# Latent attention: two heads' weighted sums side by side, probabilities scaled on GpSimd

## The reference, cut to what matters

```python
def block(i):
    start = i * ATTN_BLOCK
    ...
    s = s.astype(jnp.float32) * scale
    mask = kpos[None, :] <= qpos[:, None]
    p = jax.nn.softmax(jnp.where(mask, s, -jnp.inf), axis=-1).astype(v.dtype)
    return jnp.einsum('bqhk,bkhv->bqhv', p, v)

o = lax.map(block, jnp.arange(seqlen // ATTN_BLOCK))
...
return o @ w_o
```

## Time and profile before

| What | us |
|---|---|
| Median of 3 runs (lowest, highest) | 3575.76 (3573.05, 3577.28) |
| The profiled execution, its own time | 3576.07 |
| Its span, first to last instruction | 3574.3 |
| PE busy over the span | 3503.1 (98%) |
| DVE, ACT, POOL busy | 2034.2, 1398.5, 1637.6 |
| The loop over the items, first turn to last `turn_out` | 929.9 to 1034.0 of the span |
| In it: PE, PEld, DVE, ACT, POOL busy | 101.2, 80.2, 75.2, 65.9, 4.7 |

### The profile page before, as it was taken

One profiled execution on the slowest core, in us unless ns is written; L12 is line 12 of the kernel. 1 busy time (PEld: TensorE's weight loads), 2 busy tenths in 40 slices (PEclk: granted clock), 3 DMA queues, 4 the chain that ended last, 5 costly groups with the idle time before them and its releaser, 6 DMA issues. The chain is left out here.

```text
span 3574.3 us, 50089 instructions
## 1 busy us (share of the span) xinstructions
PE 3503.1 (98%) x17455; PEld 2955.1 (83%) x17455; DVE 2034.2 (57%) x3501; ACT 1398.5 (39%) x2168; POOL 1637.6 (46%) x814
## 2 busy tenths in 40 slices
PE   8899999999999999999999999999999999999999
PEld 6677888887788888877887788789999999788887
DVE  7835344304654430167253333379899991788887
ACT  3332532225653222223211523333359993333333
POOL 5443454344125444432442544537777776344321
PEclk9999999999999999999999999999999999999999
DMA  5122232232013323320331233236779997999997
GB/s 180 54 80 79 71 111 94 95 103 89 25 41 108 94 91 97 94 76 22 109 97 45 83 95 98 85 118 213 254 232 337 388 386 274 368 361 362 361 361 263
DMA packets 275171, 580.18 MB, mean 162 GB/s; under 512 B 119712, under 2 KB 153888, under 8 KB 273616
## 3 DMA queue, kind: packets, MB, share of 16 engines
q1 hardware_dynamic: 238160, 444.00, 37.8%
q0 software_dynamic: 36864, 134.23, 10.5%
HBM read 523.59 MB, written 54.56 MB: 162 GB/s over the span
## 5 line engine op out<-in xcount | busy, mean ns | idle before, releaser
L758 POOL TENSOR_TENSOR w_lo<-ring,w_hi 128x1024 fp32r<-128x1024 f32 (+1 forms) x159 | 413.7, 2603 | 594.2 <-ACT w_hi L710 594.2
L566 PE MATMUL ps<-h_hi,w_hi 128*128 128x512 f32 x1384 | 541.0, 391 | 2.5 <-DVE proj_ssd L873 1.3
L567 PE MATMUL ps<-h_lo,w_hi 128*128 128x512 f32 x1384 | 539.3, 390 | 0.0
L4204 POOL TENSOR_TENSOR w_lo<-ring,w_hi 128x1024 fp32r<-128x1024 f32 x142 | 358.9, 2532 | 158.1 <-ACT w_hi L4065 156.6
L4065 ACT CAST w_hi<-ring 128x1024 fp32r<-128x1024 f32 x270 | 283.1, 1049 | 321.2 <-PE ps L559 177.4
L710 ACT CAST w_hi<-ring 128x1024 fp32r<-128x1024 f32 (+1 forms) x159 | 176.9, 1112 | 582.0 <-PE ps L570 538.1
L4255 PE MATMUL ps<-h_hi,w_hi 128*128 128x384 f32 (+1 forms) x1152 | 398.5, 346 | 3.8 <-DVE h_lo L482 3.1
L4256 PE MATMUL ps<-h_lo,w_hi 128*128 128x384 f32 (+1 forms) x1152 | 393.5, 342 | 0.0
L570 PE MATMUL ps<-h_hi,w_lo 128*128 128x512 f32 x1384 | 341.7, 389 | 0.0
L4208 POOL DMA_INDIRECT xT<-in_expert_v,row_index x128 | 182.0, 1422 | 332.5 <-DVE ps L4503 317.4
L2707 POOL TENSOR_TENSOR w_lo<-ring,w_hi 128x1024 fp32r<-128x1024 f32 x84 | 209.5, 2495 | 219.9 <-ACT w_hi L2676 219.8
(11 more groups left out here) (502 smaller groups left out, 7429.0 us busy)
## 6 DMA issues: line engine op xcount, KB each, us to landing
ring<-in_expert_u SPq DMA_DIRECT2D x128, 512.0 KB
ring<-in_expert_v SPq DMA_DIRECT2D x128, 512.0 KB
ring<-in_w_gate_up SPq DMA_DIRECT2D x88, 512.0 KB
acts<-expert_gelu SPq DMA_DIRECT2D x128, 192.0 KB
gates<-peer_region SPq DMA_DIRECT2D x48, 512.0 KB
peer_region<-acts SPq DMA_DIRECT2D x128, 192.0 KB
peer_region<-gates SPq DMA_DIRECT2D x128, 192.0 KB
ring<-in_w_down SPq DMA_DIRECT2D x32, 704.0 KB
```

Source lines behind the costliest of these rows:

```text
L566: pe.matmul(out, w_hi[:, at], x_hi(k), start=start and k == 0, stop=False)
L567: pe.matmul(out, w_hi[:, at], x_lo(k), start=False, stop=False)
L758: pool.tensor_tensor(half(c.w_lo, s), raw(s), half(c.w_hi, s).bitcast(F32), ALU.subtract).then_inc(c.lo_done.sem, 1)
L4204: pool.tensor_tensor(at_slot(c.w_lo, i), at_slot(c.ring, i), at_slot(c.w_hi, i).bitcast(F32), ALU.subtract).then_inc(c.lo_done.sem, 1)
```

## The change

Items now run through two heads together: (head 2k, block i), (head 2k+1, block i), then the next block. `weigh` handles a pair of items at once: the 64 value columns are stationary, the transposed probabilities (128 columns) move, and the two heads write to the lower and the upper 64 partitions of one PSUM bank. The output is then already transposed, so `keep_out`, `heads_out` and `turn_out` are gone, and `out_high` and `out_low` read that bank. The scaling by the reciprocal moves ahead of the transpose: POOL multiplies the probabilities in SBUF, and `turn(n)` waits for it (`shared`). There are four score banks, four `probs` and four `turns` buffers, and PE, DVE and ACT work three items ahead where it was two. The two low parts of `w_o` are made by POOL behind items 8 and 12. DVE's `share` is the old `invert`, in a new place.

```diff
-    items = [(h, i) for h in range(HEADS) for i in range(NCH)]
+    items = [(2 * k + x, i) for k in range(HEADS // 2) for i in range(NCH) for x in range(2)]
...
+        probs = [c.ring[:, at:at + T] for at in (2 * T, 3 * T, SLOT + 2 * T)] + [fourth[:]]
+        turns = [turned_probs[:, r, :] for r in range(4)]
+        SCORE = (0, 1, 2, 7)
... (POOL)
+                for n in range(ni):
+                    w = (items[n][1] + 1) * P
+                    pool.wait_ge(inverted.sem, inverted.at(n + 1))
+                    pool.tensor_scalar(probs[n % 4][:, 0:w], probs[n % 4][:, 0:w], sm[:, n % 8:n % 8 + 1], None, ALU.mult
+                                       ).then_inc(shared.sem, 1)
+                    if n in (8, 12):
+                        s = n // 4 - 2
...
+                        pool.tensor_tensor(c.w_lo[:, at], c.ring[:, at], c.w_hi[:, at].bitcast(F32), ALU.subtract
+                                           ).then_inc(c.lo_done.sem, 1)
... (PE)
-                    pe.wait_ge(exp_done.sem, exp_done.at(n + 1))
+                    pe.wait_ge(shared.sem, shared.at(n + 1))
...
+                def weigh(p):
+                    k, i = p // NCH, p % NCH
+                    pe.wait_ge(turn_kept.sem, turn_kept.at(2 * p + 2))
+                    if i == 0 and k >= 2:
+                        pe.wait_ge(o_low.sem, o_low.at(k - 1))
                     for j in range(i + 1):
+                        for x in range(2):
+                            h = 2 * k + x
+                            mm = pe.matmul(c.ps[64 * x:64 * x + 64, 5 + k % 2, i * P:(i + 1) * P], v[:, j, 64 * h:64 * h + 64],
+                                           turns[(2 * p + x) % 4][:, j * P:(j + 1) * P], start=j == 0, stop=j == i)
...
+                score(2)
                 for n in range(ni):
-                    if n + 2 < ni:
-                        score(n + 2)
+                    if n + 3 < ni:
+                        score(n + 3)
                     turn(n)
...
-                    if n:
-                        weigh(n - 1)
-                    if n % 8 == 3 and n > 8:
-                        turn_out(n // 8 - 1)
+                    if n and n % 2 == 0:
+                        weigh(n // 2 - 1)
                 first_tile(1, (6,))
-                weigh(ni - 1)
-                first_tile(0, range(4))
-                turn_out(7)
-                first_tile(0, range(4, 7))
+                weigh(ni // 2 - 1)
+                first_tile(0, range(7))
... (ACT)
+                exp(2)
                 for n in range(ni):
                     keep_turn(n)
-                    if n + 2 < ni:
-                        exp(n + 2)
+                    if n + 3 < ni:
+                        exp(n + 3)
... (DVE)
+                top(2)
                 for n in range(ni):
-                    if n >= 2:
-                        invert(n - 2)
-                        keep_out(n - 2)
-                    if n + 2 < ni:
-                        top(n + 2)
-                    if n % 8 == 5 and n > 8:
+                    share(n)
+                    if n + 3 < ni:
+                        top(n + 3)
+                    if n % 8 == 2 and n > 8:
                         out_low(n // 8 - 1)
```

More of the change, by code:

```diff
@@ L2846, in latent_attention @@
         q_sq = [lat[:, k, :] for k in (0, 1, 3, 4, 5, 7)] + [tail, spare[:]]
-        probs = [c.ring[:, at:at + T] for at in (2 * T, 3 * T, SLOT + 2 * T)]
-        turns = [tail, spare[:]]
-        heads_out = [trigs[:, s, :].rearrange("p (i n) -> p i n", i=NCH) for s in range(2)]
+        fourth = c.over(c.h_lo, "probs", [P, T], F32)
+        probs = [c.ring[:, at:at + T] for at in (2 * T, 3 * T, SLOT + 2 * T)] + [fourth[:]]
+        turned_probs = c.over(c.h_hi, "turned_probs", [P, 4, T], F32)
+        turns = [turned_probs[:, r, :] for r in range(4)]
+        SCORE = (0, 1, 2, 7)
         def kept_at(x):
@@ L3007, in turn @@
                     for j in range(i + 1):
-                        mm = pe.transpose(c.ps[:, 3 + n % 2, j * P:(j + 1) * P], probs[n % 3][:, j * P:(j + 1) * P], c.ident)
+                        mm = pe.transpose(c.ps[:, 3 + n % 2, j * P:(j + 1) * P], probs[n % 4][:, j * P:(j + 1) * P], c.ident)
                     mm.then_inc(turned.sem, 1)
-                def weigh(n):
-                    h, i = items[n]
-                    pe.wait_ge(turn_kept.sem, turn_kept.at(n + 1))
-                    if n >= 2:
-                        pe.wait_ge(o_kept.sem, o_kept.at(n - 1))
+                def weigh(p):
[3 more added lines that the diff above has]
+                        pe.wait_ge(o_low.sem, o_low.at(k - 1))
                     for j in range(i + 1):
-                        mm = pe.matmul(c.ps[:, 5 + n % 2, 0:64], turns[n % 2][:, j * P:(j + 1) * P],
-                                       v[:, j, 64 * h:64 * h + 64], start=j == 0, stop=j == i)
+                        for x in range(2):
+                            h = 2 * k + x
+                            mm = pe.matmul(c.ps[64 * x:64 * x + 64, 5 + k % 2, i * P:(i + 1) * P], v[:, j, 64 * h:64 * h + 64],
+                                           turns[(2 * p + x) % 4][:, j * P:(j + 1) * P], start=j == 0, stop=j == i)
                     mm.then_inc(weighed.sem, 1)
[L3021 to L3027, removed]
                 def first_latents():
@@ L3042, in first_tile @@
                     if parts[0] == 0:
-                        pe.wait_ge(exp_done.sem, exp_done.at(ni if m == 0 else ni - 2))
+                        pe.wait_ge(exp_done.sem, exp_done.at(ni - 3 + m))
                         pe.wait_ge(c.lo_done.sem, c.lo_done.at(np_ + 5 + m))
@@ L3233, in _ @@
                         high(np_ + s, s, then[s].shape[1])
-                    if n % 8 == 4 and n > 8:
+                    if n % 8 == 1 and n > 8:
                         out_high(n // 8 - 1)
@@ L3289, in keep_value, with top, share @@
                     keep(30 + x, v[:, o % 4, o // 4 * T:(o // 4 + 1) * T], x % 4)
-                def top(n, beside=None):
+                def top(n):
                     i = items[n][1]
+                    bank = SCORE[n % 4]
                     dve.wait_ge(scored.sem, scored.at(n + 1))
-                    block_ = c.ps[:, n % 3, i * P:(i + 1) * P]
+                    block_ = c.ps[:, bank, i * P:(i + 1) * P]
                     dve.tensor_tensor(block_, block_, mat["future"], ALU.add).then_inc(masked.sem, 1)
-                    if beside is not None:
-                        invert(beside)
                     dve.wait_ge(masked.sem, masked.at(n + 1))
-                    dve.reduce_max(nm[:, n % 4:n % 4 + 1], c.ps[:, n % 3, 0:(i + 1) * P], AX.X, negate=True
+                    dve.reduce_max(nm[:, n % 4:n % 4 + 1], c.ps[:, bank, 0:(i + 1) * P], AX.X, negate=True
                                    ).then_inc(max_made.sem, 1)
-                def invert(n):
+                def share(n):
+                    i = items[n][1]
                     s = sm[:, n % 8:n % 8 + 1]
```

47 lines of the change are left out of this document (16 added, 31 removed).

## The result

| | median, us | runs (lowest to highest) | span of the profiled execution |
|---|---|---|---|
| before, beside it | 3576.08 | 4 (3573.05 to 3577.28) | 3574.3 |
| after | 3617.38 | 4 (3614.26 to 3620.22) | 3612.5 |

The changed kernel takes 1.0116 times as long (95% interval 1.0104 to 1.0129), 41 us more. The forecast was 11 us more, 3587 in a range that ended at 3601. The sign was right and the size short by 30 us.

What follows compares the result with a forecast made beforehand. Before, PE was taken as the bound, with the loop also hanging on a chain through the engines. Loop 10.7 us later, plus 0.7 for POOL's subtractions, less 0.5 behind the loop, gives 10.9 more: 3587 us, range 3577 to 3601.

Steps and rivals of the forecast that it cites:

- `share(n)` stands behind `top(n + 2)`: In DVE's queue, item n's reciprocal waits behind item n + 2's maximum, so its turn can't start sooner than C.
- the chain of even turns: In the loop: turn, `weigh`, `score`, C, next even turn; 13.29 us for two heads against 11.92.
- C: From the start of `score(n + 2)` to `turn(n)`: score to maximum's end, reciprocal, POOL; 9.04 us over four even items.
- POOL's price: POOL's scaling: 0.24, 0.41, 0.57, 0.73 us by width, sum 1.95, a third up from copy to two-input operation.
- from above: POOL's two-input operation as the upper end for its scaling: 0.50 to 1.30 us by width, sum 3.6.
- rival 1: POOL scales at the rate of two inputs: 1.65 us more for a pair, 3599 us; chance 0.17.
- the change-over: On PE, 0.15 us charged for each `weigh` for changing over, bounds 0 and 0.3; 0.60 for two heads.
- The start: Start of the loop: DVE's four norms end at 932.44, turn 0 at 933.6, next iteration at 933.7.
- The 0.5 us that was to be spared in front of L566: Behind the loop: ACT gets earlier to the next layer's pieces, which spares a wait of 0.5 us.
- Rival 3: Pipeline deep enough, PE the bound at 9.8 us: a pair 3.5 less than forecast, 3562 us; chance 0.11.
- Rival 2: POOL at the copy's rate, change-over for nothing: a pair 11.9 us as before, 3577 us; chance 0.17.
- That the 64-column matmuls would not overlap: In `weigh` on PE, 64-column matmuls don't run side by side: pair 1.9 us longer, 3600 us; chance 0.05.

Runs made afterwards that it cites:

- e6: Changed kernel with `share(n)` behind `top(n + 1)` instead of `top(n + 2)` in DVE's queue, and `out_low` two items later: 3582.38 us.
- e8: Changed kernel with one more matmul, its result unread, ahead of the wait of three turns in each pair of heads: 3612.61 us.
- e2: Changed kernel with POOL scaling only the first 128 columns of each item, the other scaling left out: 3597.35 us.
- e7: e6 with the scaling on DVE, right behind the reciprocal, instead of on POOL: 3576.96 us.
- e9: e6 with the scaling divided: POOL has the four narrow items of a pair of heads, DVE the four wide ones: 3574.22 us.
- e13: e6 with POOL scaling items 0, 1, 2, 3, 5 and DVE the others, eight buffers for turned probabilities, `weigh` for two pairs of items at once: 3571.43 us.
- e11: e6 with the scaling divided: POOL has the odd items of a pair of heads, DVE the even ones: 3573.59 us.

## Why the prediction was right in its sign and wrong in its size

**Right, and shown.** The step "`share(n)` stands behind `top(n + 2)`" and with it the chain of even turns: e6, which changes only the order of DVE's queue, takes back 35 us. The reciprocals start right behind a maximum, PE is busy 21 of 30 us, the turns wait for POOL (35.1 us in the group of L3017, where 30 were named), and at full clock `weigh` takes 1.02 us for 16 instructions (983.31 to 984.33 in e8). The hops and DVE's share of C fit within 0.1 us.

**The failed step is "POOL's price".** The prediction took 1.95 us for the four widths, a third of the way from a copy to a two-input operation. It measured 4.32, beyond the end that was called "from above" (3.6). In the chain this counts in full: 4.32 less 1.95 is 2.37 us a pair, 62% of the 3.8 by which a pair was too short (17.10 against 13.29). The reasoning "it has one large input, so I stand nearer the copy" assumed that the number of inputs sets the rate. No row showed that. The upper bound was a neighbour's price and not a bound, and rival 1, which stood on it, ended too low by 18 us for the same reason. In e2, with POOL at 602 ns for every width, 20 of the 41 us are gone.

**A term that was left out: the clock.** The prediction itself had PE idle for some 30 us, in gaps, and kept PE's and the scores' durations from rows at full clock. The granted clock fell to a mean of 0.89; e8 gives 0.68 us a pair for it.

**What is left of the pair.** 3.81 less 2.37 and 0.68 is 0.76 us. e8, where the clock is full, shows where it lies. Its four stretches C, from score to turn, are 2.41, 2.99, 3.65 and 2.94 us for items 0, 2, 4 and 6 (980.67 to 983.08, 984.33 to 987.32, 988.06 to 991.71, 992.77 to 995.71): together 11.99 against 9.04 forecast, 0.58 more than POOL's 2.37. Of that 0.38 is the score behind 64-column matmuls, whose mask starts 0.05 to 0.12 us later than the prediction had it, and the other 0.2 the hops to and from POOL. The even turns and the `weigh`s take 4.44 us, forecast 4.25: another 0.19, mostly turns that last longer ahead of a `weigh`. So the change-over was mis-sized as well, since part of it falls into C, where nothing was charged.

**The other terms.** `rest` starts at 1076.66 instead of 1046.6, 30.1 us too late. Seven pairs from the `weigh` at 936.61 to that at 1058.21 take 121.6 us, forecast 93.0, which is 28.6 of it: 7 x 3.81 = 26.7, and 1.9 for the two pairs that hold POOL's subtractions (17.8 and 18.3 us instead of 17.1; charged was 0.7, beside the 93.0). The start was 1.2 us better (turn 0 at 932.44, not 933.6, since DVE's norms came 1.6 earlier), and by difference the first and the last pair together were 2.7 worse. The 0.5 us that was to be spared in front of L566 was not: the wait of 0.51 is in the changed kernel and in each of the twelve others.

**The rivals.** Rival 3 said that PE becomes the bound once the reciprocal doesn't wait behind the maximum two items on. Its condition is what e6, e7 and e9 make true, and with it most of the loss goes (e6) or all of it (e7, e9), but the time does not fall to 3562: PE's own work is 10.6 us a pair and not 9.8, since the change-over was charged with 0.6 us a pair and costs about 1.6 (0.15 inside each of four `weigh`s and 1.0 around them). Rival 2 had the change-over for nothing and the copy's rate; both are refuted. That the 64-column matmuls would not overlap is refuted by the 1.02 us for 16.

**Where the gain on PE went.** The change removes 64 small DVE instructions that bounded nothing, the turn of the outputs (0.4 us a pair of heads) and half of `weigh`'s streaming; changing over costs nearly all that this half saved. Nor were the 11.92 us before all PE's: the score of 256 columns is followed by the turn only 0.71 us later (982.14 to 982.85), right behind the end of the exponential, where such a score alone takes 0.43, so some 0.6 us of a pair were a wait for the chain. PE's own work fell from about 11.4 to 10.6 us, and not by the 2.1 that the prediction set against 11.92. So with the chain mended and the scaling divided, a pair takes 11.3 us against 11.92; with half the change-overs and the 512-column items off POOL (e13) it takes 10.85. Seven pairs at 10.85 would give 7.5 us; the loop ends only 4.1 us sooner (L566 at 1033.89 against 1037.97), so its start and end cost 3.4, and 3.2 us are left in the medians. The loss of 41 us is a chain that the new dependence made.

**What stays open.** What lies behind the loop. In the profiled executions L566 starts 40.7 us later in the changed kernel than before (1078.69 against 1037.97), but the span is 38.2 longer; in e13 it starts 4.1 us sooner and the span, 3572.1, is 2.2 shorter; in e11 4.9 us sooner (1033.11) and the span, 3568.8, 5.5 shorter. These differences of 0.6 to 2.5 us point both ways, and executions of one and the same kernel differ by more (the kernel before by 9 us in 21 runs), so they may be nothing but that. Not tested either is why POOL's scaling is so dear: the operand per partition, the output written over the input, or the operation itself.

## What to carry to other kernels

When an instruction joins the path between two engines, read what stands ahead of it in its engine's queue: a reciprocal of 0.15 us behind somebody else's maximum cost 35 us here, and the cure was to write the loop of that queue in another order. An operation that no row shows has no price until it has run. A bound from a neighbour is no bound, and a step that hangs on it needs a range that goes past it, the more so when the operation lies in a chain, where it counts in full. And a chain that lets PE idle can cost twice: here the clock fell as well, 0.68 us of 17.1, while in e6, with shorter waits, it stayed at 1.00.

## What the runs showed of the hardware beyond what was expected

- POOL's `tensor_scalar` with one value per partition takes 603, 922, 1242 and 1562 ns for 128, 256, 384 and 512 numbers in each partition: 2.5 ns a number and 0.28 us. It is dearer than POOL's subtraction of two tensors (2348 ns for 1024 in the same kernel, 2.3 ns each in all). Every scaling was written over its input; no other form was run.
- The same operation on DVE takes 0.42 us for 384 numbers, a third of POOL's 1.24, but 2.60 us when POOL's subtraction of 2.34 us starts within 0.05 us of it. Beside POOL's own `tensor_scalar` it was at most 0.15 us longer (0.59 us for 512 numbers instead of 0.49, once 0.50 for 256 instead of 0.35).
- 64-column matmuls of two halves run side by side at 0.22 to 0.24 us a block of both heads, where 128-column ones take 0.20 for one head; going over to them and back costs about 0.4 us each time.
- TensorE's granted clock had a mean of 0.89 in a stretch in which PE was busy 71% of the time with single gaps of 1.2 to 1.9 us, falling to a mean of 0.57 over 3 us soon behind the longest of them, and 1.00 with an unused matmul in three of the gaps of each pair (82% busy).
